# Loading the rows of x in halves of 64 partitions, from two queues, in a hybrid encoder kernel

## The reference

```
h = rmsnorm(x, norm_pre)                    # per row: x * rsqrt(mean(x*x) + eps) * gain
proj = h @ w_in                             # 2048 x 15504: branches A, B, C and merge gates
ya = mLSTM(pa); yb = HGRN2(pb); yc = RWKV-7(pc)   # recurrences over the rows, with states
merged = ga*(ya@w_proj_a) + gb*(yb@w_proj_b) + gc*(yc@w_proj_c)
x' = x + rmsnorm(merged @ w_out, norm_post)
```

## Time and profile before

| what | us |
|---|---|
| median of 3 executions (2358.94 to 2360.14) | 2359.89 |
| the profiled execution | 2361.02 |
| its span, first to last instruction | 2358.4 |
| PE busy in it | 2302.1 (98%) |
| first product (L937) begins at | 25.58 |

### The profile page before, as it was taken

How to read it: one execution, slowest core, us unless ns; L and a number is a source line. 1 busy time by engine, 2 the same in 40 slices (tenths; PEclk the granted TensorE clock), 3 DMA queues, 4 the chain that set the end, 5 groups by cost and what they waited for, 6 DMA issues and landing times.

```text
span 2358.4 us, 46095 instructions
## 1 busy us (share of the span) xinstructions
PE 2302.1 (98%) x19261; PEld 2221.8 (94%) x19261; DVE 1289.9 (55%) x1966; ACT 790.9 (34%) x1179; POOL 47.9 (2%) x71
## 2 busy tenths in 40 slices
PE   6999999999999999999999999999999999999998
PEld 5999999999999999989989989999999999999998
DVE  4444434487767776636526427455656664445354
ACT  5312221234333333324234233243334343325443
POOL 0010001000000000000000000000000000000000
PEclk9999999999999999999999999999999999999999
DMA  5322122133343343112112121131212245344465
GB/s 168 114 80 81 69 81 79 66 100 118 107 138 108 122 138 152 52 45 89 49 47 103 47 73 54 48 141 60 95 72 78 87 137 192 132 149 175 146 205 187
DMA packets 64151, 246.64 MB, mean 105 GB/s; under 512 B 8723, under 2 KB 16069, under 8 KB 45637
## 3 DMA queue, kind: packets, MB, share of 16 engines
q1 hardware_dynamic: 64020, 244.69, 29.9%
HBM read 214.49 MB, written 30.17 MB: 104 GB/s over the span
## 4 chain that ended last, share of the span: by engine, by line
PE 84%; DVE 7%; issue 3%; DMA 3%; ACT 2%; SPq 1%; DVEq 0%; POOL 0%; ACTq 0%; POOLq 0%
PE acc L937 47%; PE acc L1095 10%; PE acc L1464 6%; PE branch L1095 5%; PE branch L1189 2%; PE branch L1464 2%; PE branch L1227 2%; DMA w_raw<-in_w_stream 1%; DVE w_lo L1972 1%; ACT w_hi L1511 1%; PE branch L1182 1%; PE branch L1372 1%; DMA scratch<-in_x_all 1%; PE branch L1040 0%; DVE scratch L2361 0%
## 5 line engine op out<-in xcount | busy, mean ns | idle before, releaser
L937 PE MATMUL acc<-act_hi,w_hi 128*128 128x320 f32 (+3 forms) x3328 | 1018.7, 306 | 9.7 <-DVE w_lo L1972 7.3
L937 PE MATMUL acc<-act_lo,w_hi 128*128 128x320 f32 (+3 forms) x3328 | 987.2, 297 | 0.0
L937 PE MATMUL acc<-act_hi,w_lo 128*128 128x320 f32 (+3 forms) x3328 | 986.7, 296 | 0.0
L937 PEld LDWEIGHTS acc<-act_hi,w_hi 128*128 128x128 f32 x3328 | 628.1, 189 | 26.3 <-DVE w_lo L1972 8.8
L937 PEld LDWEIGHTS acc<-act_lo,w_hi 128*128 128x128 f32 x3328 | 628.1, 189 | 0.7
L937 PEld LDWEIGHTS acc<-act_hi,w_lo 128*128 128x128 f32 x3328 | 627.6, 189 | 0.0
L1972 DVE TENSOR_TENSOR w_lo<-w_raw,w_hi 128x2048 fp32r<-128x2048 f32 x135 | 309.1, 2290 | 280.5 <-ACT w_hi L1511 279.9
L1511 ACT ACTIVATE w_hi<-w_raw 128x2048 fp32r<-128x2048 f32 x135 | 258.7, 1916 | 177.8 <-PE branch L1464 118.3
L1464 PE MATMUL acc<-act_lo,w_hi 128*128 128x288 f32 x384 | 113.2, 295 | 0.0
L1464 PE MATMUL acc<-act_hi,w_hi 128*128 128x288 f32 x384 | 113.0, 294 | 0.0
L1464 PE MATMUL acc<-act_hi,w_lo 128*128 128x288 f32 x384 | 112.9, 294 | 0.0
(11 more groups left out here) (445 smaller groups left out, 3286.8 us busy)
## 6 DMA issues: line engine op xcount, KB each, us to landing
w_raw<-in_w_stream SPq DMA_DIRECT2D x136, 1024.0 KB, 4.9
w_raw<-in_w_stream SPq DMA_DIRECT2D x68, 512.0 KB, 5.9
gate_logits<-gate_out SPq DMA_DIRECT2D x48, 288.0 KB, 2.1
scratch<-gate_logits SPq DMA_DIRECT2D x48, 288.0 KB, 3.1
scratch<-in_x_all SPq DMA_DIRECT2D x9, 512.0 KB, 5.9
branch_rows<-branch_out SPq DMA_DIRECT2D x16, 288.0 KB, 2.2
scratch<-in_x_all SPq DMA_DIRECT2D x3, 1024.0 KB, 10.0
out_y_prompt<-scratch SPq DMA_DIRECT2D x6, 512.0 KB, 2.9
```

Of the source, the lines that this page charges most:

```text
L937: last = mm(acc[s][:, at:at + hi - lo], a[:, s, w], b[:, k, lo:hi], start=(k == order[0] and a is whi and b is xh), stop=(k == order[-1] a ...
```

## The change

`given` also cuts at partition 64, so that every tile has a lower piece (partitions 0 to 63) and an upper one. SP asks only for the pieces that begin below partition 64. The upper ones (four of 64 rows, one of 16) are asked for by ACT as its first five instructions, ahead of its table load and of its waits. The semaphores and what waits for them stay; `X_LOADS` is now 2 for each tile.

```
-                lo, hi = max(a, P * t), min(b, P * t + rows)
-                if lo < hi:
-                    pieces.append((lo - P * t, hi - P * t, x_all[at + lo - a:at + hi - a, :]))
+                for c in (P * t, P * t + P // 2):
+                    lo, hi = max(a, c), min(b, P * t + rows, c + P // 2)
+                    if lo < hi:
+                        pieces.append((lo - P * t, hi - P * t, x_all[at + lo - a:at + hi - a, :]))
...
                 for a, b, src in given(t, ROWS[t]):
-                    sp.dma_start(xt[a:b, t, :], src).then_inc(x_here[t], 16)
+                    if a < P // 2:
+                        sp.dma_start(xt[a:b, t, :], src).then_inc(x_here[t], 16)
...
+            for t in range(5):
+                for a, b, src in given(t, ROWS[t]):
+                    if a >= P // 2:
+                        act.dma_start(xt[a:b, t, :], src).then_inc(x_here[t], 16)
             nc.scalar.preload_act_table_set("exp_and_others")
```

## The result

The change makes the kernel slower: 2369.20 us median of 6 executions (2365.83 to 2371.66) against 2360.01 of 6 (2358.07 to 2363.23), a ratio of 1.0033 with a 95% interval of 1.0022 to 1.0044. Timed again, 11 executions against 33, it was 2367.83 against 2361.46, ratio 1.0025, 1.0016 to 1.0034. A loss of 5.2 to 8.0 us lies in both intervals. The prediction was 2361.9, +2.0, with 2365.8 as its upper end; the measured time lies above that.

The account below looks back on a forecast made before the run. The fifth x tile's landing at the start was taken to bound the kernel: its square 2.0 us later, weight transfers hidden, first-matmul changes taken as 0, gave 2361.9 by the median. Forecast's own range 2360.5 to 2364.0; full range 2356.2 to 2365.8.

Parts of the forecast that it names:

- What bounds the kernel: At the start, the fifth tile's landing sets the first product; a microsecond there is a microsecond of the total.
- my own sign (1.3 us): Carrying the fifth square over is wrong if the total moves by over 1.3 us other than that square does.
- Issuing costs nothing: ACT's five new requests before its first square hold it 2.5 to 3.0 us, covered by its idleness.
- Stage (2): With `full` in SP's queue, packet turns let eight upper rows go alone: 5.6 us, to 10.4 us.
- (1): Tile 0 at the start: some 9 rows for each engine, both halves busy, 2.8 us, to 4.8 us.
- (3): After `full`: tile 1's lower rows beside the last upper ones, 8 x 0.31 = 2.5 us, to 12.9.
- (4): ACT's queue empty: lower halves of tiles 2, 3 and 4 go alone, 7.4 us, to 20.3 us.
- my 21.7: Forecast start in us of the fifth square, held by the fourth square on ACT; 2.0 us later than 19.74.
- Rival B: Moving x: every row at the slow rate, fifth square 3.7 to 6.2 us later, middle total 2364.9; chance 0.22.
- turns by whole piece: A reason for the 0.22 rival: engines alternate queues by whole pieces, so all 16 write one half; x ends 22.9 to 25.4.
- engines in step: The 0.22 rival's other reason: all engines move the same half together, some 220 GB/s instead of 412.
- 0.65 of the chance: Forecast's 0.38 and 0.27 for a rival: halves mix finely, queues in step, fifth square 2.9 to 3.3 us sooner, 2356.8.

Follow-up runs that it names:

- same half: Cut rows, two queues, `full` last, against the change: both queues hold lower halves, then upper halves, together; fifth square 27.56, total 9.4 us above before's single 2359.48.
- 8 rows ahead: Change with `full` last, and ACT first asks for 8 rows into memory nothing reads; fifth square 25.20, total 8.7 us above before's single 2359.48.
- behind the table load: Change with `full` last, ACT's five requests placed behind `preload_act_table_set`, though the first began beside it; fifth square 25.43, total 5.7 us above before's single 2359.48.
- tiles 0 and 4 whole: Against before, one queue: source rows reordered so tile 0 is one piece, tile 4 one piece of 80 rows; -2.5 us, ratio 0.9987.
- the change again: The changed kernel, unaltered, timed once more against before; fifth square 27.13, +6.4 us, ratio 1.0025.

## Why the prediction was wrong

- *What bounds the kernel.* Right. In all twelve kernels profiled the first product follows the fifth square by 5.8 to 5.9 us, and in each row of the table the shift of the first product lies in the interval of the total. By my own sign (1.3 us) the first median was too far off, 9.2 against a shift of 6.9; the second was not, 6.4 against 7.4. The three kernels timed once (same half, 8 rows ahead, behind the table load) lie 1.6, 3.1 and 0.0 us above their shifts.
- *Issuing costs nothing.* Right: 3.25 us on ACT, with 3.15 us of idleness left behind it before the first square.
- *Stage (2), the turns.* The mechanism was right for this stage, and its length too (`full`'s rows go from about 7.6 to 12.7 us, 5.1 against 5.6). At the start it was not so: tile 0's halves did not take turns row by row. The gap before the second square was to be over 5 us and is 8.01; the packets of the two queues are equal in number, and with `full` moved away the gap is 3.43. It is worth 2.3 us of the end.
- *Stages (1) and (3), "both halves busy".* This step failed. I let a row take 0.31 us in both, the rate of the earlier trace rows's tiles 1 to 3, because both queues would hold opposite halves. In (1) the halves went one after the other, and `full`'s rows began at 7.6 us instead of 4.8. Side by side would not have helped: with the 8 rows ahead the two halves of tile 0 were, at 227 GB/s. In (3) opposite halves were side by side, and the rate was 244 GB/s (12.5 to 17 us), 0.54 us for a row. By the packets of the trace, `full` is moved from 7.6 to 12.7 us, ACT's last row begins at 17.1, and SP's last row of x ends at 25.1. So the stages took, against the forecast: (1) 5.6 us for 2.8, (2) 5.1 for 5.6, (3) 4.4 for 2.5, (4) 8.0 for 7.4. Together that is 4.8 of the 4.9 us by which the fifth square missed my 21.7. The lines for (3) and (4):

```profile
12.50:17.00 4.50, 0.47 (x1) 0.18 (x1) 0.32 (x1) 0.00 (x0) 0.00 (x0) 1.00 1.04 244
17.10:25.00 7.90, 0.48 (x1) 0.18 (x1) 2.01 (x2) 5.14 (x5) 1.50 (x4) 1.00 1.02 204
```

- *The choice among cases.* Rival B, with 0.22, had named this rate, its place and its price (every row at the slow rate, fifth square 3.7 to 6.2 us later); it is 6.9. Its two reasons fare worse: turns by whole piece are seen only at the start, and the 8 rows ahead speak against engines in step; B's rate is shown, its cause is not. I held against B that the slow rate had been seen only where the other half wasn't to be had. The rows had shown full rate in one situation alone, 128-row pieces; that two halves from different requests would do the same was nowhere in them, and I gave it 0.65 of the chance. The Trainium skill (DMA: Bandwidth & Descriptors, section Rules for kernel authors) advises one 128-partition transfer instead of two halves; the trace agrees, with 220 GB/s against 412.
- *The range.* It took B as high as 5.9 us but not to its own end of 6.2, and left nothing for a step worse than computed or for the spread of medians (9.2 and 6.4 for the same kernel).

## What to carry to other kernels

Ask for rows in pieces that lie across partition 64, best in whole tiles of 128; look for a low GB/s at full busy share, and mend it by laying out the source so that a tile is one piece. A second queue adds no rate to whole tiles and some 7% to halves, and once both queues have rows waiting each gets an equal number of packets, not of bytes: a transfer of small rows in one queue lets the other run ahead by whole pieces. Where work follows tile by tile, the order of landing counts beside the end of moving.

## What the runs showed beside this

Single executions of the same kernel differ by up to 10 us (2354.64 to 2364.97 with tiles 0 and 4 whole, 2364.66 to 2372.92 for the change again), and one place of it was seen. The change's second profile has a span of 2370.3 against 2363.9, with a first product only 0.5 us later. At 1930 us the two are 0.9 us apart, at the last store 6.4. Between lies this (the second profile, then the first; the number before the last two is the granted clock):

```profile
1945.00:1955.00 10.00, 7.23 (x34) 7.23 (x35) 5.03 (x6) 2.30 (x2) 0.00 (x0) 0.66 0.68 246
```

```profile
1945.00:1955.00 10.00, 10.00 (x77) 10.00 (x78) 4.01 (x5) 3.23 (x2) 0.00 (x0) 1.00 0.74 277
```

PE had waited 3.0 us for DVE there instead of 1.1, and was then granted 0.50 of the clock, 1.2 GHz, from 1948 to 1952 us, and 1.00 again from 1954; the profile has 34 matmuls in the ten microseconds instead of 77. Why the wait was longer this time was not followed, nor whether such falls make the 9.2 of the first median.
